# A hybrid attention and retention layer: x laid out by columns too, and a new order at the start

## The reference

```python
u = rms_norm(h, norm_gain[layer])
z = jnp.einsum('bsd,de->bse', u, w_in[layer])
...
y_a = dsa_attention(q_a, k_a, v_a, q_i, k_i, w_i, topk) * jax.nn.silu(g_a)
y_r = retention(q_r, k_r, v_r) * jax.nn.silu(g_r)
h = h + jnp.einsum('bse,ed->bsd', jnp.concatenate([y_a, y_r], -1), w_out[layer])
...
return rms_norm(h, final_gain)
```

## Time and profile before

| what | value |
|---|---|
| median of 3 runs | 304.5 us |
| lowest, highest | 302.53, 304.65 us |
| span of the profiled execution | 300.2 us |
| median of the runs less that span | 4.3 us |
| TensorE (PE) busy | 288.5 us, 96% of the span |
| VectorE (DVE) busy | 204.2 us, 68% |
| ScalarE (ACT) busy | 146.3 us, 49% |
| POOL busy | 71.6 us, 24% |
| mean granted clock of TensorE | 0.989 of full speed |
| moved by DMA | 28.01 MB |

### The profile page before, as it was taken

The page is one execution under the profiler, slowest core; times in us unless marked ns, Lnnn a source line. Parts: engine busy times, 40 slices in busy tenths (PEclk is TensorE's granted clock), DMA queues, the critical chain, the costliest instruction groups (busy, mean ns, idle before and its releaser), DMA issues.

```text
span 300.2 us, 4549 instructions
## 1 busy us (share of the span) xinstructions
PE 288.5 (96%) x1551; PEld 246.4 (82%) x1551; DVE 204.2 (68%) x434; ACT 146.3 (49%) x328; POOL 71.6 (24%) x133
## 2 busy tenths in 40 slices
PE   7898999999999999997999999999999999999992
PEld 6898888888878888886888888798888888888891
DVE  1884788999999999559984862638646525843441
ACT  4876764532735525562566444465442671441231
POOL 0066742363310029991200002010010020000111
PEclk9799999999999999999999999999999999999997
DMA  6852650053044054040304220030210315411113
GB/s 234 300 226 72 209 145 1 0 157 125 14 141 127 2 151 130 1 140 3 102 37 142 70 70 0 4 140 4 75 64 2 90 52 178 170 35 39 71 76 134
DMA packets 14230, 28.01 MB, mean 93 GB/s; under 512 B 1016, under 2 KB 2560, under 8 KB 14208
## 3 DMA queue, kind: packets, MB, share of 16 engines
q1 hardware_dynamic: 13632, 26.95, 27.7%
q10 hardware_dynamic: 576, 0.79, 0.7%
HBM read 25.63 MB, written 2.10 MB: 92 GB/s over the span
## 4 chain that ended last, share of the span: by engine, by line
PE 74%; DVE 12%; issue 3%; ACT 2%; POOL 0%; DVEq 0%; ACTq 0%; POOLq 0%
PE bank L389 18%; PE bank L391 18%; PE bank L390 18%; PE bank L434 6%; DVE keys L940 4%; DVE top L938 3%; PE bank L448 3%; DVE w_lo L857 3%; PE bank L462 2%; PE bank L475 2%; PE bank L463 2%; DVE k_stack L902 1%; PE bank L496 1%; PE bank L509 1%; PE bank L410 1%
## 5 line engine op out<-in xcount | busy, mean ns | idle before, releaser
L389 PE MATMUL bank<-w_hi,xT_hi 128*128 128x512 f32 (+2 forms) x328 | 127.4, 388 | 2.7 <-DVE w_lo L857 1.9
L391 PE MATMUL bank<-w_hi,xT_lo 128*128 128x512 f32 (+2 forms) x328 | 124.3, 379 | 0.0
L390 PE MATMUL bank<-w_lo,xT_hi 128*128 128x512 f32 (+2 forms) x328 | 124.1, 378 | 0.0
L389 PEld LDWEIGHTS bank<-w_hi,xT_hi 128*128 128x128 f32 x328 | 62.0, 189 | 14.1 <-issue 3.1
L391 PEld LDWEIGHTS bank<-w_hi,xT_lo 128*128 128x128 f32 x328 | 61.9, 189 | 11.4
L390 PEld LDWEIGHTS bank<-w_lo,xT_hi 128*128 128x128 f32 x328 | 62.1, 189 | 9.9
L857 DVE TENSOR_TENSOR w_lo<-w_raw,w_hi 128x1024 fp32r<-128x1024 f32 (+1 forms) x40 | 47.4, 1204 | 14.3 <-ACT w_hi L559 14.1
L559 ACT ACTIVATE w_hi<-w_raw 128x1024 fp32r<-128x1024 f32 (+1 forms) x40 | 40.3, 1023 | 5.1 <-PE bank L391 3.2
L667 ACT ACTIVATE work<-work,small 128x128 f32<-128x128 f32 (+3 forms) x32 | 17.8, 556 | 34.7 <-DVE small L963 34.7
L806 POOL TENSOR_TENSOR th<-zt,tab 128x64 f32<-128x64 f32 (+2 forms) x32 | 16.6, 519 | 59.1 <-ACT zt L600 56.1
L762 POOL TENSOR_SCALAR small<-small 128x1 f32<-128x1 f32 (+1 forms) x8 | 2.7, 343 | 106.7 <-ACT junk L688 92.6
(11 more groups left out here) (103 smaller groups left out, 342.3 us busy)
## 6 DMA issues: line engine op xcount, KB each, us to landing
w_raw<-in_w_in SPq DMA_DIRECT2D x28, 512.0 KB, 3.6
w_raw<-in_w_out SPq DMA_DIRECT2D x8, 512.0 KB, 3.7
retT<-in_x SPq DMA_DIRECT2D x8, 256.0 KB, 4.0
x_h<-in_x SPq DMA_DIRECT2D x3, 512.0 KB, 5.7
w_raw<-in_w_in SPq DMA_DIRECT2D x4, 324.0 KB, 4.7
out<-x_h SPq DMA_DIRECT2D x4, 320.0 KB, 2.5
out<-x_h ACTq DMA_DIRECT2D x4, 192.0 KB, 2.7
tab<-in_table SPq DMA_DIRECT2D x1, 691.0 KB, 7.1
```

The costliest lines, as they stand in the source:

```text
L389: pe.matmul(o, xh, hi[:, kk, c0:c0 + w], start=first, stop=False)
L390: pe.matmul(o, xh, lo[:, kk, c0:c0 + w], start=False, stop=False)
L391: mm = pe.matmul(o, xl, hi[:, kk, c0:c0 + w], start=False, stop=last)
```

## The change

The host passes two more arrays: `x_cols`, x with its columns on the partitions, and `gain_cols`, the gain in the same way. SP and ScalarE's queue load x_cols into `mix` (free at that time) and `xT_hi` and `xT_lo` are made from there; blocks 2 and 3 are handled together, 256 wide. TensorE's transposes of x and of the gain are gone. x by rows is still loaded for the squares. The order of the first loads is new, the table comes in two parts, and ScalarE's queue issues two of the loads. In groups 0 to 3 the two hi times hi matmuls of a unit come first and wait for the hi parts alone; these groups use four PSUM banks. The transposes of zt, with their evacuation and lo part, follow three slots behind their group (`LAG`) instead of two, with three zt buffers; index logits and scores and the top-k rounds begin one slot later. Warm-up matmuls: 10 instead of 7.

```diff
+LAG = 3
-TOPK0 = 5
+TOPK0 = 6
-WARM_UP = 7
+WARM_UP = 10
...
+def x_columns(x):
+    return x[0].reshape(MT, P, KT, P).transpose(3, 0, 2, 1).reshape(P, MT * KT * P)
+def x_ops(m, k):
+    return min(m, 2) * KT + k + 1
...
     if slot < MT:
-        units = {(2, "middle"): [u, u + 1], (3, "middle"): [u + 2, u + 3]}
+        units = {(1, "middle"): [u, u + 1], (2, "middle"): [u + 2], (2, "end"): [u + 3]}
...
-        n = min(4 if g <= 8 else 3 if g <= 12 else 2, ROUNDS * (MT - 1) - done)
+        n = min(4 if g <= 9 else 3 if g <= 13 else 2, ROUNDS * (MT - 1) - done)
...
+        def proj_bank(g):
+            return bank[g] if g < MT else proj_ps[g % 2]
+        def x_piece(m, k):
+            if m < 2:
+                return xT_raw[:, m, k, :], slice(m * P, (m + 1) * P)
+            return xT_raw[:, 2:4, k, :], slice(2 * P, 4 * P)
...
+            def load_unit(u):
...
+            sp.dma_start(x_flat[:, 0:KQ * P], x_cols[:, 0:KQ * P]).then_inc(xT0_first, 16)
+            load_unit(0)
+            load_unit(1)
+            load_unit(2)
+            sp.dma_start(x_flat[:, KT * P:2 * KT * P], x_cols[:, KT * P:2 * KT * P]).then_inc(xT1_in, 16)
+            load_unit(3)
+            load_x(0)
+            sp.dma_start(tab[:, 0:TAB_EARLY], table[:, 0:TAB_EARLY]).then_inc(tab_early_in, 16)
+            sp.dma_start(x_flat[:, 2 * KT * P:], x_cols[:, 2 * KT * P:]).then_inc(xT23_in, 16)
+            load_x(1)
+            load_unit(4)
+            load_unit(5)
+            load_x(2)
+            load_unit(6)
+            load_unit(7)
+            load_x(3)
+            sp.dma_start(tab[:, TAB_EARLY:], table[:, TAB_EARLY:]).then_inc(tab_in, 16)
+            for u in range(2 * QS, UNITS):
+                load_unit(u)
...
-            pe.transpose(mid_ps[:, 0:KT], gain_rows, ident[0:KT, 0:KT]).then_inc(gain_t, 1)
-            def transpose_x(m):
...
-                    if 2 <= g < MT * C_RG + 2:
+                    if MT <= g < MT + 2:
+                        pe.wait_ge(z_done, g - MT + 1)
+                    elif MT + 2 <= g < MT * C_RG + 2:
                         pe.wait_ge(z_done, g - 1)
...
-                if g < MT:
-                    pe.wait_ge(xlo_done, KT * g + KQ * (q + 1))
-                pe.wait_ge(wlo_done, u + 1)
+                if g < MT:
+                    pe.wait_ge(xhi_done, x_ops(m, KQ * q + KQ - 1))
+                    pe.wait_ge(whi_done, u + 1)
+                    for kk in range(KQ):
+                        k = KQ * q + kk
+                        pe.matmul(o, xT_hi[:, k, t], hi[:, kk, c0:c0 + w], start=k == 0, stop=False)
+                    pe.wait_ge(xlo_done, x_ops(m, KQ * q + KQ - 1))
+                pe.wait_ge(wlo_done, u + 1)
...
                 if i == 0:
-                    pe.wait_ge(xlo_done, 2 * KT)
+                    pe.wait_ge(ident_done, 1)
...
-                transpose_group(g - 2)
+                transpose_group(g - LAG)
...
-                if MT <= g < 2 * MT - 1:
-                    index_logits(g - MT + 1)
+                if MT < g < 2 * MT:
+                    index_logits(g - MT)
...
+            act.dma_start(gain, gain_cols).then_inc(gain_in, 16)
+            act.dma_start(x_flat[:, KQ * P:KT * P], x_cols[:, KQ * P:KT * P]).then_inc(xT0_rest, 16)
...
+            act.wait_ge(xT1_in, 16)
             x_hi(1)
             square_x(0)
-            square_x(2)
-            x_hi(2)
+            act.wait_ge(xT23_in, 16)
+            x_hi(2, range(0, KH))
...
-                transposed_out(g - 2)
+                transposed_out(g - LAG)
                 for u in splits_at(g, "middle"):
+                    split_hi(u)
+                if g == 2:
+                    square_x(2)
+                for u in splits_at(g, "end"):
                     split_hi(u)
                 if g < GROUPS:
                     project_out(g)
                 if g == 0:
-                    x_hi(3)
+                    x_hi(2, range(KH, KT))
...
             x_lo(1)
+            x_lo(2)
             square_x(1)
-            x_lo(2)
-            square_x(3)
-            x_lo(3)
...
-                if 0 <= g - 2 < MT:
-                    index_lo(g - 2)
-                if 0 <= g - 2 - 2 * MT < MT:
-                    key_lo(g - 2 - 2 * MT)
-                for u in splits_at(g, "middle"):
+                if 0 <= g - LAG < MT:
+                    index_lo(g - LAG)
+                if 0 <= g - LAG - 2 * MT < MT:
+                    key_lo(g - LAG - 2 * MT)
+                for u in splits_at(g, "middle") + splits_at(g, "end"):
                     split_lo(u)
+                if g == 2:
+                    square_x(3)
```

More of the change, by code:

```diff
@@ L155, in transposed, with hymba_layer @@
     return g if c < 3 else g - MT
-def hymba_layer(nc, x, norm_gain, w_in, w_out, final_gain, table, out):
+def hymba_layer(nc, x, w_in, w_out, final_gain, table, x_cols, gain_cols, out):
     with ExitStack() as ctx:
@@ L206, in hymba_layer @@
         st_sb = sb("st_sb", [P, RH * P])
-        state = zt[:, :, :].rearrange("p n (a e) -> p n a e", a=2)
+        state = zt[:, 0:2, :].rearrange("p n (a e) -> p n a e", a=2)
+        squares = v_ret[:, :, :].rearrange("p (i a) c -> p i (a c)", i=2)
         small = sb("small", [P, 128])
-        gain_rows = st_sb[0:KT, 0:P]
         gain = small[:, 0:8]
@@ L378, in proj @@
                         pe.wait_ge(mixlo_done, 2 * (m + 1))
-                if g < MT:
-                    pe.wait_ge(xlo_done, KT * g + KQ * (q + 1))
-                pe.wait_ge(wlo_done, u + 1)
-                o = proj_ps[g % 2][:, 0:w]
+                o = proj_bank(g)[:, 0:w]
                 hi = w_hi[:, u % RING, :].rearrange("p (k c) -> p k c", k=KQ)
                 lo = w_lo[:, u % RING, :].rearrange("p (k c) -> p k c", k=KQ)
+                t = slice(m * P, (m + 1) * P)
+                if g < MT:
[6 more added lines that the diff above has]
+                pe.wait_ge(wlo_done, u + 1)
                 for kk in range(KQ):
                     k = KQ * q + kk
[L387 to L391, removed]
+                    if g >= MT:
+                        pe.matmul(o, xT_hi[:, k, t], hi[:, kk, c0:c0 + w], start=k == 0, stop=False)
+                    pe.matmul(o, xT_hi[:, k, t], lo[:, kk, c0:c0 + w], start=False, stop=False)
+                    mm = pe.matmul(o, xT_lo[:, k, t], hi[:, kk, c0:c0 + w], start=False, stop=k == KT - 1)
                 if q == QS - 1:
@@ L874, in square_x @@
                 dve.wait_ge(x_loaded[m], 16)
-                dve.tensor_tensor_reduce(out=mix[:, m, :], in0=x_in[:, m, :], in1=x_in[:, m, :], scale=1.0 / D_MODEL,
+                dve.tensor_tensor_reduce(out=squares[:, 1, :], in0=x_in[:, m, :], in1=x_in[:, m, :], scale=1.0 / D_MODEL,
                                          scalar=0.0, op0=ALU.mult, op1=ALU.add, accum_out=ssq[:, m:m + 1]).then_inc(sq_odd, 1)
@@ L1126 @@
     arrays["table"] = tables()
+    arrays["x_cols"] = np.ascontiguousarray(x_columns(np.asarray(inputs["x"])))
+    arrays["gain_cols"] = np.ascontiguousarray(gain_columns(np.asarray(inputs["norm_gain"])))
     args = [nc.dram_tensor(f"in_{n}", a.shape, mybir.dt.from_np(a.dtype), kind="ExternalInput").ap()
```

120 lines of the change are left out of this document (47 added, 73 removed).

## The result

The changed kernel takes 310.28 us (median of 4 runs, 309.21 to 311.31); the kernel before, with one run more on the same chip, 303.51 us (302.44 to 304.65). The ratio is 1.024, with an interval of 1.020 to 1.027: slower. The profiled execution took 310.86 us with a span of 309.0, so 1.9 us lie around the span, and 1.8 in the other three. The span of 300.2 in the table before therefore belongs to an execution of about 302 us, one near the lowest of its runs, and of the 8.8 us between the two spans some 2 are spread between runs; the medians differ by 6.8.

What follows compares the result with a forecast made beforehand. TensorE and VectorE were near-bounds; the ScalarE-POOL loop (rstd, z, rope) held the start. Terms -0.6 +1.5 +1.1 +1.5 = +3.5 on span 300.2 gave 303.7, with 4.3 around it 308.0 us; range 300.8 to 310.3.

Steps and rivals of the forecast that it cites:

- Part 1: Start, x transposes and first loads: group 0 at about 6.5 us, group 4 at 24.4; worth 4.8 us by itself.
- Part 2: Later zt transposes (LAG 3): those in mid slot 4 wait for z(2) and run at 31.4 us; gain of 0.6 us.
- Part 3: Clock after TensorE's idle from 27.2 to 31.4 us: lower level for some 3 us of work, 1.5 us lost.
- Part 4: VectorE's top-k stage: scores and rounds one slot later make the third key_lo late; +1.1 us, between 0 and 1.6.
- Part 5: Last two top-k rounds, ending in slot 23, delay `ret_kv(0)`: +1.5 us, between 0 and 1.9.
- (a): Start gains its best, ScalarE never kept by POOL, late terms hold: -1.1 us, 303.4 us; chance 0.18.
- (b): TensorE bounds all, VectorE's own pauses take up its lag: -3.7 us, 300.8 us, down to 299.7; chance 0.15.
- (c): The 1 MB (x blocks 2 and 3) lands 1.5 us later, z(0) to z(2) with it: 309.5 us; chance 0.10.
- (d): Stages after group 4 wait for what they waited for before, nothing moves: 303.5 to 305.5 us; chance 0.10.

Runs made afterwards that it cites:

- 1: Changed kernel with ScalarE's evacuations of transposed groups 0, 1 and 2 (and their lo parts) moved ahead in its order: 302.69 us, ratio 0.999 to the kernel before.
- 2: Changed kernel with 25 spare identity matmuls filling TensorE's pause in the middle of slot 4: 308.01 us, ratio 1.017 to the kernel before.
- 3: Changed kernel with the top-k rounds back at slots 5 to 22, scores still one slot later: 308.15 us, ratio 1.017 to the kernel before.
- 4: Kernel before with only the top-k rounds moved one slot later (slots 6 to 23): 304.92 us, ratio 1.005.
- 8: Changed kernel with the edit of 1 and 3 rounds in slots 17 and 18, so rounds end in slot 22: 302.07 us, ratio 0.996.
- 11: Kernel of 6 with the second part of x block 0 (384 KB) moved from ScalarE's queue to SP's, behind unit 0: 302.69 us, ratio 0.997.
- 12: Kernel of 7 with the second part of x block 0 (384 KB) moved from ScalarE's queue to SP's, behind unit 0: 302.62 us, ratio 0.999.
- 9: Changed kernel with LAG back at 2 and all else kept: 310.64 us, ratio 1.022 to the kernel before.
- 10: Changed kernel with VectorE waiting for rstd(1) and rstd(2) before the splits of units 4 and 7: 309.66 us, ratio 1.022.
- 5: Changed kernel with the edits of 1 and 3 together: 301.61 us, ratio 0.995 to the kernel before.
- 6: Kernel of 5 with fewer top-k rounds in slots 10 to 13 and more in slots 14 and 15: 303.42 us, ratio 0.998.
- 7: Kernel of 6 with 3 top-k rounds in slots 14 and 16 to 19 instead of 4 and 3 in 14 and 15: 304.19 us, ratio 1.002.

## Why the prediction was right in its direction and short in its size

**The mechanisms.** The pause before the second zt transposes, its releaser, the low clock behind it, the small waits for `k_stack` and the wait for `st_sb` before `ret_kv(0)` all came where the prediction put them. Experiments 1 and 2 take the pause and the low clock away, and 3, 4 and 8 show that the wait for `st_sb` is the rounds' end. The small waits for `k_stack` are where they were forecast, but what makes them was not isolated (see experiment 4).

**Part 1 was too good by about 1 to 2 us.** Unit 0's split was at 6.7 us, and the first matmul at 7.59 instead of 6.5: unit 0 comes later while ScalarE's queue loads too, as 11 and 12 show. Unit 3's was at 11.68, not 10.4, and the 1 MB was there at 17.0, not 15.1. z(0) ended at 19.2 (17.7 predicted) and group 4 began at 26.12 (24.4).

**Part 2 is the term that failed.** It said -0.6 us and was +3.0, 3.6 of the 5.3 us by which the sum was short on the spans. The logic, that the middle of slot 4 waits for z(2), was right; the moment of z(2) was 32.6 us and not 29.7. The 3.6 us of error (34.97 against 31.4) can be followed step by step. VectorE's square of block 1 ended at 22.7 instead of 21.0: 1.7, part 1's lateness carried on. From there to z(1) it was 3.7 us against 3.6, though the first rstd step took 1.13 us: what was predicted for this stretch held. From z(1) (26.4, 24.6 predicted) to z(2) it was 6.2 us against 5.1: here I had put the neighbour's work on the power operation alone, and the rows show one step of the rotation at 1.25 us and the scaling after the second power at 0.70 as well. The last 0.7 lie behind z(2): 2.4 us to the transposes against 1.7, where my own steps ended at 31.8 and I took 31.4. So about half of the error is the late start, a third the POOL steps, and most of the rest my rounding down. The part also laid the loss on the lag, and 9 shows the same time with the old lag. What I hadn't done was to ask whether the evacuation must stand there at all; 1 shows that its place is worth 7.6 us, more than the whole predicted loss.

**Part 3** had 1.5 us, and 2 measured 2.0 to 2.3. I took 3 us of work at the lower clock, and it was 4.7 (35.0 to 39.6). In 3 and 10 it was about 3, and the loss 1.4: half of the work's length fits all three, and the length is what I had too short. That an idle of under 2 us costs no clock, as the part says, isn't safe either: the last section has a fall behind 1.98 us.

**Part 4** had +1.1, and from slot 8 to slot 20 the change lost 1.3. In it are the wait for `w_lo` of 0.4 in slot 16, which I hadn't listed, and the longer road through slots 12 to 14. **Part 5** had +1.5, and the wait was 1.47 us. From slot 20 to `ret_kv(0)` the loss is 2.0, though, and 0.5 more follows to the end. The first 0.45 of this is the one zt transpose group more that part 4 had counted: behind slot 20's start the kernel after has two (147.99 and 155.24 us), the kernel before one (141.69). Of the last 0.5, 0.37 come just behind `ret_kv(0)` and go with the late rounds, as experiment 8 shows; 0.1 stays unexplained.

**The sum.** Predicted -0.6, 1.5, 1.1 and 1.5; measured on the spans 3.0, 2.0, 1.3 and 2.0, with 0.5 at the end: 8.8 against 3.5. The predicted time came out nearer (308.0 against 310.28) only by luck: by the 4.3 us that I put around a span, where every execution of the two kernels listed here has 1.7 to 1.9. A forecast of 303.7 + 1.8 = 305.5 is what my terms said of that execution. The 4.3 held the spread of the runs, which belongs to the median and not to the frame of one execution.

**The rivals.** (a), the start at its best with the late terms kept, named the rows of experiment 1: transposes at 28.3 us (28.48 measured), no low clock, 303.4 us (302.69). The rows are the mechanism; the time is partly the same 4.3 us, since by its terms the span was 299.1 and it is 300.3. (b) asked VectorE to take up its own lag, and 5 to 8 show that it doesn't: in the best of them, 5, a lead of 3.0 us in slot 4 (29.00 against 31.96) becomes 1.3 us at the end (301.61 against 302.94 of the kernel before beside it). (c), the late 1 MB, was in part true, 1.9 us late instead of 1.5, and its 309.5 us came nearest; but moving the evacuation alone takes 7.6 us off though the 1 MB lands at 16.2 us there, still later than predicted, so it isn't what made the kernel slower. (d), that nothing moves behind group 4, is refuted by the table.

## What to carry to other kernels

Before a removed piece of work is credited, walk each in-order queue past the moved step and ask what the item ahead of it waits for: here an evacuation whose input had been ready for 8 us stood behind one that waited for POOL, and its place alone was worth 7.6 us. Work out the serial loop between the slower engines (sum of squares, POOL's rstd, z, rotation) first, with every step of it at its length beside the neighbour's work; the matmul engine's saving only counts where that loop isn't the limit. Where two engines are both near their bounds, moving the second's load from one stretch to another moved the wait (k_stack, w_lo, slot 20) and hardly shortened it, so the saved TensorE time came back as 1.3 us of some 5. And look at the clock behind each wait before two placings are compared: in three traces a wait of 2.0 to 3.1 us was followed by 0.50 and cost 1.6 us more than its own length.

## What the runs showed that was not expected

- Waiting out the mutual exclusion of VectorE and POOL didn't remove it: the split that was held back cost the rotation 1.25 us twice where the power operation had lost 0.8. The Trainium skill, SBUF — State Buffer, section "Who interferes with whom", says that a VectorE instruction with two SBUF inputs contends with a GpSimd instruction that reads SBUF, and that the shared port pair is an exclusive lock. The 1.25 us of a POOL step that takes 0.27 alone, beside a split of 1.2 us, agree.
- A pause of 6 us on TensorE cost 2.0 to 2.3 us more behind it: the clock of 0.50 lasted from about 32.8 to 39.6 us, 4.7 of them with work. Filling the pause with useless transposes made the kernel faster.
- Waits of 2 to 3 us can bring the low clock too. It fell behind 1.98 us in slot 20 (6), 2.03 in slot 16 (11) and 3.11 in slot 20 (12), each time for 1.6 us of loss, and not behind 2.25 in slot 20 (7), 2.00 there (9) or 2.03 in slot 16 (6). These runs don't tell what decides it.
- A transfer of 384 KB on a second queue moved the landing of the first weight unit on the other from 4.3 to 6.1 us.
